# GpSimd multiplies and ScalarE sums a quarter of the expert dots in the two middle phases of a hybrid decoder trunk

## The reference

```
best_s, best_pos = lax.top_k(cand_s, PEER_TOPK)
idx = jnp.take_along_axis(cand_i, best_pos, axis=-1)
gate = jax.nn.softmax(best_s, axis=-1)
u = expert_u[idx]
act = jax.nn.gelu(jnp.einsum('nhkd,nd->nhk', u, xb), approximate=False)
coef = (gate * act).astype(xb.dtype)
return jnp.einsum('nhk,nhkd->nd', coef, expert_v[idx])
```

## Time and profile before

| | us |
|---|---|
| median of 3 runs | 1666.14 (1664.14 to 1669.15) |
| the profiled execution's own time | 1660.97 |
| its span, first to last instruction | 1659.1 |
| PE busy | 1198.7 (72%) |
| DVE busy | 1191.4 (72%) |
| ACT busy | 496.1 (30%) |
| POOL busy | 588.6 (35%) |
| bytes moved by DMA | 665.99 MB, mean 401 GB/s |

### The profile page before, as it was taken

The page is one execution under the profiler, slowest core; times in us unless marked ns, Lnnn a source line. Parts: engine busy times, 40 slices in busy tenths (PEclk is TensorE's granted clock), DMA queues, the critical chain, the costliest instruction groups (busy, mean ns, idle before and its releaser), DMA issues.

```text
span 1659.1 us, 21548 instructions
## 1 busy us (share of the span) xinstructions
PE 1198.7 (72%) x7384; PEld 576.7 (35%) x7384; DVE 1191.4 (72%) x3414; ACT 496.1 (30%) x1139; POOL 588.6 (35%) x525
## 2 busy tenths in 40 slices
PE   7776876767848975986796698688697855655555
PEld 3463222214514652432263266444235411111111
DVE  3366867866668877887574887889947677777755
ACT  0122225222223442562132344255212222222211
POOL 1033333534434233333233433232333344444451
PEclk9888987888968997997998699899798976778886
DMA  9569999999999999999999999999999999999996
GB/s 382 233 258 422 422 422 420 407 424 421 421 422 397 423 424 400 375 426 400 417 400 421 417 423 424 422 420 414 379 395 403 421 421 421 422 420 421 421 421 254
DMA packets 83788, 665.99 MB, mean 401 GB/s; under 512 B 9344, under 2 KB 9488, under 8 KB 10592
## 3 DMA queue, kind: packets, MB, share of 16 engines
q0 software_dynamic: 74608, 540.65, 79.1%
q1 hardware_dynamic: 8928, 123.46, 17.7%
q10 hardware_dynamic: 144, 0.52, 0.1%
HBM read 663.55 MB, written 1.05 MB: 401 GB/s over the span
## 4 chain that ended last, share of the span: by engine, by line
DMA 33%; DVE 27%; PE 26%; issue 6%; ACT 5%; POOL 2%; DVEq 0%; POOLq 0%; SPq 0%; ACTq 0%; PEldq 0%
DMA ring<-in_experts,idx 31%; PE acc L824 12%; DVE ring L1397 9%; PE act_bank L533 6%; PE dve_bank L519 5%; DVE scratch L1048 3%; DMA scratch<-in_bias 2%; POOL ring L465 2%; ACT L859 2%; DVE onehot L1048 2%; ACT diag L999 1%; DVE scratch L1212 1%; ACT scratch L859 1%; DMA wbuf<-in_weights 1%; PE act_bank L805 1%
## 5 line engine op out<-in xcount | busy, mean ns | idle before, releaser
L465 POOL DMA_INDIRECT ring<-in_experts,idx x512 | 582.7, 1138 | 1024.3 <-PE acc L824 792.8
L824 PE MATMUL acc<-ring,diag 64*64 64x512 f32 x4096 | 625.9, 739 | 365.9 <-ACT diag L999 353.5
L1397 DVE CUSTOM_DVE_ANT_0 ring<-ring,hn 128x1024 f32<-128x1024 f32 x512 | 621.6, 1224 | 222.2 <-DMA ring<-in_experts,idx 205.8
L824 PEld LDWEIGHTS acc<-ring,diag 64*64 64x64 f32 x4096 | 155.8, 156 | 733.4 <-ACT diag L999 491.7
L992 ACT ACTIVATE acts<-dots 128x2 f32<-128x2 f32 x256 | 52.0, 203 | 700.8 <-DVE dots L1397 699.6
L533 PEld LDWEIGHTS act_bank<-hnT,wbuf 128*128 128x128 f32 x1856 | 215.7, 194 | 58.0 <-issue 57.7
L533 PE MATMUL act_bank<-hnT,wbuf 128*128 128x128 f32 x1856 | 229.0, 280 | 8.7 <-ACT scratch L859 8.4
L999 ACT ACTIVATE diag<-cst,coefs 128x64 f32<-128x64 f32 x512 | 150.2, 340 | 250.1 <-DVE coefs L1405 239.2
L859 ACT ACT_TABLE_LOAD x80 | 102.6, 1283 | 12.2 <-DMA rowc<-in_rows 9.7
L1405 DVE TENSOR_TENSOR coefs<-acts,gate 128x2 f32<-128x2 f32 x256 | 41.2, 161 | 82.7 <-ACT acts L992 73.7
L992 ACT ACT_TABLE_LOAD x68 | 87.2, 1283 | 7.3 <-DVE dots L1397 1.2
(11 more groups left out here) (138 smaller groups left out, 923.7 us busy)
## 6 DMA issues: line engine op xcount, KB each, us to landing
wbuf<-in_weights SPq DMA_DIRECT2D x51, 2048.0 KB, 12.4
ring<-in_weights SPq DMA_DIRECT2D x5, 2048.0 KB, 32.5
ring<-in_experts,idx POOLq DMA_INDIRECT x512, 15.8
kept<-in_weights SPq DMA_DIRECT2D x2, 2048.0 KB, 33.6
scratch<-in_bias POOLq DMA_DIRECT2D x1, 1024.0 KB, 29.1
out<-h SPq DMA_DIRECT2D x2, 512.0 KB, 5.3
scratch<-in_bands POOLq DMA_DIRECT2D x1, 768.0 KB, 16.9
h<-in_x SPq DMA_DIRECT2D x1, 512.0 KB, 4.1
```

The lines of the kernel that those rows point to most:

```text
L465: pool.indirect_dma_start(ring[:, n % RING], None, io[f"experts{layer}"], bass.IndirectOffsetOnAxis(idx[:, at:at + 1], 0),).then_inc(sem(f ...
L824: last[rows] = pe.matmul(acc[rows][half][home:home + HALF_P], diag[part, n % DIAGS], ring[part, slot, D + half * CW:D + (half + 1) * CW], ...
L1397: dve.tensor_tensor_reduce(out=ring[:, slot, 0:D], in0=ring[:, slot, 0:D], in1=hn[:, phase % NBLK], scale=1.0, scalar=0.0, op0=ALU.mult, o ...
```

## The change

Of every four slots in phases 1 and 2 the last (n % 4 = 3) is **shared**: 64 slots of 512. DVE skips its dot. POOL multiplies its U half with `hn` into the same place of the ring. ACT sums the products with a Copy that has an accumulator output into the same column of `dots`, before the pair's Gelu. The multiply of slot n stands in POOL's queue behind the gather of slot n+6 (`POOL_BEHIND`). ACT waits for the product, sums it, waits for its own sum, then waits for the other dot of the pair, then takes the Gelu. Nothing changes in phases 0 and 3, in PE's order or in SP's.

```diff
+SHARED_PHASES, SHARED_EVERY = (1, 2), 2 * GROUP
+POOL_BEHIND = 6
+def by_pool(n):
+    return n // SLOTS in SHARED_PHASES and n % SHARED_EVERY == SHARED_EVERY - 1
...
-            for n in range(PHASES * SLOTS):
-                gather(n // (NBLK * SLOTS), n)
+            def multiply(n):
+                slot = n % RING
+                pool.wait_ge(sem(f"rows_in{slot}"), 16 * (n // RING + 1))
+                pool.tensor_tensor(ring[:, slot, 0:D], ring[:, slot, 0:D], hn[:, n // SLOTS % NBLK],
+                                   ALU.mult).then_inc(sem("products_made"), 1)
+
+            for n in range(PHASES * SLOTS + POOL_BEHIND):
+                if n < PHASES * SLOTS:
+                    gather(n // (NBLK * SLOTS), n)
+                if n >= POOL_BEHIND and by_pool(n - POOL_BEHIND):
+                    multiply(n - POOL_BEHIND)
...
-                act.wait_ge(sem("dot_done"), g * BODY + (q + 1) * GROUP)
+                at = g * BODY + q * GROUP
+                for n in range(at, at + GROUP):
+                    if by_pool(n):
+                        act.wait_ge(sem("products_made"), POOL_DOTS[n + 1])
+                        rows = ring[:, n % RING, 0:D]
+                        lane(act.activation(rows, rows, ACT.Copy, accum_out=dots[:, n % BODY:n % BODY + 1]))
+                act.wait_ge(sem("dot_done"), VECTOR_DOTS[at + GROUP])
                 act.activation(acts[:, cols], dots[:, cols], ACT.Gelu).then_inc(sem("gelu_done"), 1)
...
                 at = g * BODY + n
+                if by_pool(at):
+                    return
                 slot = at % RING
```

More of the change, by code:

```diff
@@ L105 @@
 ASKED_BY = 121
+SHARED_PHASES, SHARED_EVERY = (1, 2), 2 * GROUP
+POOL_BEHIND = 6
+def by_pool(n):
+    return n // SLOTS in SHARED_PHASES and n % SHARED_EVERY == SHARED_EVERY - 1
+VECTOR_DOTS, POOL_DOTS = [0], [0]
+for _n in range(PHASES * SLOTS):
+    VECTOR_DOTS.append(VECTOR_DOTS[-1] + (not by_pool(_n)))
+    POOL_DOTS.append(POOL_DOTS[-1] + by_pool(_n))
 HALF_P = P // 2
```

## The result

The changed kernel takes **1728.3 us** (median of 4 runs, 1724.98 to 1729.66) against 1666.86 (1664.14 to 1669.15) for the kernel before: ratio 1.0372, 95% interval [1.0358, 1.0387], 61.4 us slower. The forecast was 1679, its range 1655 to 1709. The profiled execution took 1724.98 (span 1723.1), so 64 us above the one of before.

A forecast was written before the change was run, and what follows sets the result against it. Bound: bytes at 421 GB/s plus 21 us of dry DMA queue in phases 1 and 2. Late products +13, relief -6, port +6 gave +13, 1674 profiled, 1679 us with the 5.2 median offset; range 1655 to 1709.

The forecast's parts named there:

- A change of engines can move only the second part: Whole kernel: time is bytes at 421 GB/s plus dry-queue time; only the dry 21 us of phases 1 and 2 can be won.
- the relief: DVE, phases 1 and 2: each skipped dot saves 1.14 us; counted at 11 in-time pairs, about half, -6 us.
- The prices: Each shared slot: POOL multiply 2.45 us, ACT sum 1.26; a 1.28 us table load moves onto the path in 32 pairs.
- The one-time cost: POOL's first multiply: an extra ISA instruction might cost a few us once; given no case of its own.
- Most of that is hidden under the DMA queue: Phases 1 and 2: most of the shared pairs' 122 us of lateness costs nothing, since the DMA queue covers it.
- The 122 us of lateness: Shared pairs, phases 1 and 2: 43 of 64 have coefficients later than in the old timeline, by 122 us in sum.
- 24 bare places of 64: Shared pairs with a nearby gather landing under 10 us after issue; 13 late, 26.5 us left after deductions, half counted: +13.
- a loop that breaks more than once a pair: Case left outside the range 1655 to 1709 that was to hold 8 in 10.
- The port term: DVE, phases 1 and 2: multiplies keep out two-input operations, 0.46 x 2.45 = 1.1 us each, at 11 in-time pairs, half counted: +6.
- The rival with "the port held": POOL's multiply takes 3.67 us and shuts DVE out; 18 bare pairs late, +42, 1708 us; chance 0.15.
- Coefficients waiting over 100 us: Sign in the changed profile: the wait of DVE's coefficients for ACT's Gelu rises from 44.7 us to over 100.
- If DVE's dots keep 1.22 us throughout, the port term is 0: Sign in the changed profile: unchanged dots mean no port cost; a rising mean of dots or two-input operations makes it real.

The follow-up runs named there:

- e16: Changed kernel with the multiply cut from 1024 to 64 columns and placed four slots behind instead of six; 1651.22 us, 14.9 under the kernel before.
- e8: Changed kernel with the multiply of slot n behind gather n+4 instead of n+6; 1683.74 us, 17.8 above the kernel before.
- e11: Kernel before, all dots on DVE, plus 64 POOL multiplies of constants that nobody waits for, four slots behind; 1721.74 us, +55.5.
- e9: The change made in phase 3 alone, 32 shared slots, multiply six slots behind; 1711.72 us, 45.5 above the kernel before.
- e13: The change in phase 3 alone, 32 shared slots, multiply four slots behind instead of six; 1668.57 us, 3.1 above the kernel before.
- e3: Kernel before without DVE's 64 shared dots, plus 64 POOL multiplies of constants that nobody waits for, no sums; 1699.49 us, +34.1.
- e1: Changed kernel without multiplies and sums, the 64 shared dots left out altogether; 1650.14 us, 15.3 under the kernel before.
- the memsets: Kernel before, all dots on DVE, plus eight POOL memsets of 128 columns at each of the 64 places; 1669.54 us, +3.6.
- the copy: Kernel before, all dots on DVE, plus one single-input POOL copy of 1024 columns of constants at each of the 64 places; 1692.99 us, +26.8.
- e10: Changed kernel with the multiply four slots behind and the Gelu's table loaded ahead of the wait for the product; 1687.42 us, +21.2 against before.
- e14: Kernel before, all dots on DVE, plus 32 POOL multiplies of constants that nobody waits for, in phase 3 alone; 1667.85 us, +2.3.

## Why the prediction was off

**The bound and the relief.** "A change of engines can move only the second part", 21 us, held for what can be won: the best run won 15.3. The relief was priced at -6, half-counted, and is -15.3: DVE was the late one in nearly all dry time, not in half of it. I had read PE as late too (18.6 of 20 busy in one stretch); but e16's phase 1, shown above, gives PE as much work (332.5 us of 430) at 420 GB/s, so PE alone leaves nothing dry.

**The prices.** Multiply 2.36 (taken 2.45), sum 1.06 with 0.19 for the read (taken 1.26), table load 1.28 in the loop: all right. The Trainium skill's price in "GPSIMD Engine Reference", section "Elementwise — side-by-side cycle accounting", gave an estimate of 2.25; the trace has 2.36. The one-time cost that I had thought possible isn't there: the first multiply takes 2.35 and starts 0.1 us behind the gather before it.

**The step that failed** is "Most of that is hidden under the DMA queue". The 122 us of lateness stand as a sum laid against the timeline of before (POOL's gathers and DVE's coefficients alone, without the landings, give 94 us if no pair has a table load and 144 if all have). But that timeline has each pair start anew at its old time. In truth a late pair's sum releases the gathers in front of the next shared multiply, so the lateness is handed on every four slots. A deep queue hides a delay that comes once; against turns of 11.8 us where the DMA wants 9.96 (phase 3), or 14.3 where it wants 12.8 (phases 1 and 2), it only puts off the loss. I counted 24 bare places of 64 and got +13. The runs show 44 us for the place of the multiply (e8), of which up to 21 may be the port's (e11), and 42 us in 32 slots where I would have counted almost no bare place (e9 less e13; the least time to landing there was 9.9 us before). My text had set this case aside as "a loop that breaks more than once a pair". The period could have been worked out beforehand. From the gather's start to the coefficients it is 2 x 0.94 + 0.30 + 2.45 + 1.26 + 0.28 = 6.17 us. The way from there through diagonals and 16 matmuls to the next gather stands in phase 3 of the kernel before:

```profile
1441.92 0.16 DVE L1405 TENSOR_TENSOR coefs<-acts,gate 128x2 f32<-128x2 f32 x1 [0.27 <-ACT acts L992]
...
1447.30 0.94 POOL L465 DMA_INDIRECT ring<-in_experts,idx  x1 [4.86 <-PE acc L824]
```

That is 5.38 us, so an estimate of 11.55 us a turn with nothing else in the queues, against the DMA's 9.96; the side work of phases 1 and 2 comes on top.

**The port term** was mis-sized by far: +6, and measured 49 (e3 against e1), or at most 33 with the loop open (e8 against e16). Two parts of it were wrong. The size: 1.1 us a multiply from "0.46 x 2.45", measured 1.38. I let only the large two-input operations count; the trace shows the coefficients of two columns and TENSOR_SCALARs held just as long. Against e1, which lacks the same 64 dots, the changed kernel's coefficients are busy for 17 us more and its TENSOR_SCALARs of scratch, `expd`, `gate` and `pos_hi` for 35, together more than half of the 88.5; its dots are for 2.6. The places: I counted it at 11 pairs, halved. DVE's queue does not forget a loss at a late pair, and it bears it at 64. The rival with "the port held" ended at 1708 and named both causes; its 3.67 us multiply was wrong, and it too counted each delay once.

"SBUF — State Buffer", section "Who interferes with whom", in the Trainium skill says more than I used: besides two-input instructions it lists copy, cast and tensor_scalar as ops that can enter a mode in which they take the shared ports, and it exempts GpSimd instructions that only write from the clash with two-input ones. The trace agrees with the first (646 ns for a 356 ns TENSOR_SCALAR) and nearly with the second (the memsets cost 3.6 us, with 12 us more on DVE, where the copy has 48). It also agrees with the rule that an operation with one SBUF input outside such a mode doesn't contend (the searches, last section).

**What I said would show it.** Coefficients waiting over 100 us: yes, 139.9. ACT waiting for the product: yes. GB/s under 409 and 412: yes, 380. "If DVE's dots keep 1.22 us throughout, the port term is 0" was a bad test: their mean is 1232 ns, and the loss lies in the small operations around the multiply. The second half of that sign, a rise in two-input operations, did come (161 to 229 ns).

**The terms together.** Relief -15.3, port +49.4 (e3 against e1), product's path +27.3 (the rest, e3 to the change): +61.4. In the other order: -14.9 (e16), +32.7 for the multiply with the loop open, +43.6 for the closed loop, again 61.4. The split between the two depends on the order: the 43.6 may hold up to 21 of the port's (e11), and a slow DVE may also lengthen the loop, which no run shows. In either order the path, which I had at +13, is 27 to 44 us, the port, which I had at +6, is 33 to 49, and the relief, which I had at -6, is 15. The relief, undersized as well, took some of the error back by luck.

## What to carry to other kernels

Where a step waits for the end of its own earlier turn, write the loop down and compare its period with the pace of what it feeds; lateness against the old timeline doesn't give the period, and a deep queue only delays the loss. Place a helper's work so that it depends on an older turn: here one pair more of distance was worth 44 us, and behind it a shorter path (e10) brought nothing. And before work goes from VectorE to GpSimd, count VectorE's loss for every such instruction, small operations included: in this change it was 1.38 us against a relief of 1.14.

## What the runs showed of the hardware

An operation of 16 columns can be held for a whole multiply; this is e13 in phase 3:

```profile
1459.30 2.36 POOL L488 TENSOR_TENSOR ring<-ring,hn 128x1024 f32<-128x1024 f32 x1 [2.38 <-DMA ring<-in_experts,idx]
1459.46 2.22 DVE L1386 TENSOR_TENSOR pos_f<-pos_f 128x16 f32<-128x16 f32 x1
```

The searches (MAX8, FIND_INDEX8, MATCH_REPLACE8) are not held. In e14 they run at their usual length under a multiply. The multiply itself is 0.28 us longer than its 2.35 here, where a dot was running when it came:

```profile
1400.16 1.22 DVE L1428 CUSTOM_DVE_ANT_0 ring<-ring,hn 128x1024 f32<-128x1024 f32 x1 [0.83 <-DMA ring<-in_experts,idx]
1400.96 2.63 POOL L489 TENSOR_TENSOR ring<-cst 128x1024 f32<-128x1024 f32 x1
...
1401.77 0.28 DVE L1338 FIND_INDEX8 top_i<-top_s,scores 128x8 uint32<-128x128 f32 x1
...
1402.29 0.27 DVE L1339 MATCH_REPLACE8 scores<-top_s,scores 128x128 f32<-128x128 f32 x1
...
1402.74 0.47 DVE L1340 MAX8 top_s<-scores 128x8 f32<-128x128 f32 x2
```

The held coefficients of the first timeline had started 0.58 us ahead of the multiply, under the gather before it, and were held all the same. They are no single case: at 964.63 in the same trace the coefficients start 0.59 us ahead of a multiply and take 2.97 us. Why an instruction that was first lost its turn stays open.

TensorE's clock takes part as well. Two pairs in the timeline of the changed kernel:

```profile
508.06 3.69 PE L848 MATMUL acc<-ring,diag 64*64 64x512 f32 x16 [6.62 <-ACT diag L1029]
...
512.85 1.95 PE L848 MATMUL acc<-ring,diag 64*64 64x512 f32 x16
```

The same 16 matmuls take 3.69 us at a granted clock of 0.50 (1.2 GHz), behind 6.6 us without work, and 1.95 at 1.00 (2.4 GHz), right behind other matmuls. In e9's loop PE stands 6.0 us and takes 3.69 again. Of an 11.4 us turn 1.7 us are thus an estimate of the lower clock's share. The kernel before pays them in phase 3 too (3.69 us at 1442.75), where the deep queue hides them; in a closed loop they are on the path.
